# Adding the last pair's expert results with a gated selection matrix, and loading the gathered rows in two halves

## What is computed

```python
h = layer_norm(ALPHA * h + mix, ln_g[i, 0], ln_b[i, 0])        # layers 0 and 1
ffn = hier_moe(h, ...)      # gate_k * (silu(x @ w_gate[e_k]) * (x @ w_up[e_k])) @ w_down[e_k], k = 0, 1
h = layer_norm(ALPHA * h + ffn, ln_g[i, 1], ln_b[i, 1])
...
x = x + concat([att, lru_out]) @ w_out                         # layer 2
x = x + hierarchical_moe(rmsnorm(x, ffn_norm), ...)
return rmsnorm(x, final_norm)
```

## Time and profile before

| | us |
|---|---|
| median of 3 runs | 2155.4 (2151.24 to 2159.71) |
| profiled execution | 2147.33 |
| its span, first to last instruction | 2145.5 |
| PE busy in it | 1970.6 (92%) |
| DVE, ACT, POOL busy | 678.6, 404.3, 119.2 |
| mean granted clock of PE, 1 being 2.4 GHz | 0.968 |

### The profile page before, as it was taken

How to read it: one execution, slowest core, us unless ns; L and a number is a source line. 1 busy time by engine, 2 the same in 40 slices (tenths; PEclk the granted TensorE clock), 3 DMA queues, 4 the chain that set the end, 5 groups by cost and what they waited for, 6 DMA issues and landing times.

```text
span 2145.5 us, 25273 instructions
## 1 busy us (share of the span) xinstructions
PE 1970.6 (92%) x10013; PEld 1052.8 (49%) x10013; DVE 678.6 (32%) x1617; ACT 404.3 (19%) x873; POOL 119.2 (6%) x142
## 2 busy tenths in 40 slices
PE   8999989999999997799999999999499989999883
PEld 4444445555455453645545545544444445665442
DVE  0155547221111111535421111111637223532123
ACT  1033432111111111111111111111233222112112
POOL 0000001000000000000100000000010001111100
PEclk9999999999999999899999999999799999999997
DMA  9511103899999999722899999999821111699994
GB/s 318 152 57 40 40 20 114 356 419 420 420 421 421 420 419 372 273 83 79 313 419 420 421 420 421 421 419 404 287 84 40 39 40 41 217 366 418 419 419 200
DMA packets 122049, 593.93 MB, mean 277 GB/s; under 512 B 15915, under 2 KB 41403, under 8 KB 58991
## 3 DMA queue, kind: packets, MB, share of 16 engines
q1 hardware_dynamic: 108495, 565.96, 66.4%
q0 software_dynamic: 13472, 26.84, 3.8%
HBM read 573.48 MB, written 35.44 MB: 284 GB/s over the span
## 4 chain that ended last, share of the span: by engine, by line
PE 78%; DMA 14%; DVE 4%; ACT 2%; issue 1%; SPq 0%; DVEq 0%; POOLq 0%; ACTq 0%
PE bank L946 21%; PE bank L627 10%; PE bank L986 10%; PE bank L869 9%; DMA ring<-in_w_up_dram 6%; DMA ring<-in_moe_w_up_dram 6%; PE bank L769 4%; PE bank L639 4%; PE bank L613 3%; PE bank L1112 1%; PE bank L723 1%; PE bank L696 1%; PE bank L1073 1%; PE bank L860 1%; PE bank L683 1%
## 5 line engine op out<-in xcount | busy, mean ns | idle before, releaser
L946 PE MATMUL bank<-ring,work 128*64 128x512 f32 (+1 forms) x3008 | 562.5, 526 | 29.0 <-DMA ring<-in_w_up_dram 25.5
L946 PEld LDWEIGHTS bank<-ring,work 128*64 128x64 f32 x3008 | 224.8, 138 | 362.8 <-issue 335.3
L986 PE MATMUL bank<-ring,work 128*64 128x512 f32 x1280 | 295.9, 600 | 5.3 <-DVE work L1748 5.3
L1748 DVE COPY work<-bank 128x256 f32<-128x256 f32 (+1 forms) x96 | 36.5, 380 | 703.7 <-PE bank L861 703.7
L869 PE MATMUL bank<-work 128*128 128x128 f32 x2048 | 245.7, 278 | 0.0
L627 PE MATMUL bank<-hT,ring 128*128 128x512 f32 x512 | 236.9, 605 | 0.7 <-ACT work L1175 0.7
L869 PEld LDWEIGHTS bank<-work 128*128 128x128 f32 x2048 | 233.5, 192 | 6.1 <-issue 2.0
L1264 ACT ACTIVATE work<-bank 64x512 f32<-64x512 f32 x96 | 56.6, 589 | 540.8 <-PE bank L986 540.8
L986 PEld LDWEIGHTS bank<-ring,work 128*64 128x64 f32 x1280 | 84.3, 136 | 145.3 <-issue 129.1
L627 PEld LDWEIGHTS bank<-hT,ring 128*128 128x128 f32 x512 | 94.0, 193 | 109.1 <-issue 107.3
L1254 ACT ACTIVATE work<-bank 64x512 f32<-64x512 f32 (+1 forms) x96 | 49.7, 517 | 477.2 <-PE bank L946 477.2
(11 more groups left out here) (291 smaller groups left out, 1632.2 us busy)
## 6 DMA issues: line engine op xcount, KB each, us to landing
ring<-in_moe_w_down_dram SPq DMA_DIRECT2D x128, 1024.0 KB, 16.5
ring<-in_moe_w_gate_dram SPq DMA_DIRECT2D x126, 1024.0 KB, 15.4
ring<-in_moe_w_up_dram SPq DMA_DIRECT2D x126, 1024.0 KB, 17.2
ring<-in_w_down_dram SPq DMA_DIRECT2D x32, 1024.0 KB, 26.1
ring<-in_w_gate_dram SPq DMA_DIRECT2D x31, 1024.0 KB, 23.0
ring<-in_w_up_dram SPq DMA_DIRECT2D x31, 1024.0 KB, 24.9
ring<-in_attn_w_qkv_dram SPq DMA_DIRECT2D x12, 1024.0 KB, 13.7
work<-y_rows SPq DMA_DIRECT2D x12, 1024.0 KB, 8.0
```

Of the source, the lines that this page charges most:

```text
L946: mm = pe.matmul(GU2[s % 2][BLK * a:BLK * a + BLK, 0:F], xgT[pair % 2][:, per * kk + k, BLK * of_pair:BLK * of_pair + BLK], v[a][:, k, :], ...
L986: mm = pe.matmul(DN[BLK * n:BLK * n + BLK, :], hT_[:, 2 * kk + k, :], v[:, k, 512 * n:512 * n + 512], start=(kk + k == 0), stop=(2 * kk + ...
```

## The change

The results of the last two experts (30 and 31) are no longer stored to `y_rows`.

- ACT writes them to `last_y`, 128 rows by 1024. DVE builds a selection matrix for this pair, `last_sel`, whose entries are the gates (`select_last`, in slot 27); PE turns it (`turn_last_selection`, slot 29, four transposes); DVE copies it to `last_sum`. After the last expert PE computes for each tile two matmuls of 128 by 512 columns (`sum_last_pair`), and DVE adds them to `h` from the banks (`add_last`). The gates of choices that went to this pair are set to zero in `wts`; `y_rows` is filled with zeros once at the start, 4 MB.
- SP loads tiles 0 and 1 of the rows when the first 15 pairs' stores have landed, then issues the next projection's four units, then loads tiles 2 and 3. In layer 2 all four tiles are loaded in one go at that point.
- `project_turned` issues the sums of tiles 0 and 1 ahead of its loop, those of tiles 2 and 3 after the projection of tiles 0 and 1. ACT's order is not touched.
- DVE combines tiles 0 and 1 first, then adds the last pair tile by tile.
- In layer 2 the last pair's rows are gathered by matmuls like those of the first pairs, since the gated selection needs the selection matrix; `over_slots` has one turn ahead of its loop and two behind it in all layers.
- Two parameter semaphores are joined into one.

```diff
@@ load_tiles, after_gather (SP)
+            sp.dma_start(y_rows.rearrange("(p n) (q c) -> p (n q) c", p=P, c=256),
+                         zeros[:, :].unsqueeze(1).to_broadcast([P, 2 * S // P * 4, 256])).then_inc(rows_zeroed, 16)
...
-            def load_tiles(l):
+            def load_tiles(l, tiles):
                 sp.wait_ge(over_moved, l + 1)
-                for y_stored in steps.y_stored:
-                    sp.wait_ge(y_stored, 16 * (E // 4) * (l + 1))
-                for tt in range(T):
+                for y_stored, n in zip(steps.y_stored, STORES):
+                    sp.wait_ge(y_stored, 16 * n * (l + 1))
+                for tt in tiles:
...
-            def after_gather(l, u0, u1):
-                load_tiles(l)
+            def after_mixture(l, u0, u1, u2):
+                load_tiles(l, range(2))
+                for u in range(u0, u1):
+                    load(u)
+                load_tiles(l, range(2, T))
                 for tt in range(T):
                     sp.wait_ge(routing.gathered[tt], 16 * (l + 1))
-                for u in range(u0, u1):
+                for u in range(u1, u2):
                     load(u)
...
-            for u in range(first["pin"], first["pgrp"]):
-                load(u)
-            after_gather(0, first["pgrp"], first["moe1"])
+            after_mixture(0, first["pin"], first["pgrp"], first["moe1"])
@@ PE
+            def sum_last_pair(l, tt):
+                for n in range(2):
+                    mm = pe.matmul(last_bank(l, tt, n)[:, :], last_sum[:, P * tt:P * tt + P],
+                                   last_y[:, 512 * n:512 * n + 512], start=True, stop=True)
+                mm.then_inc(last_added, 1)
...
+            def project_turned(l, name, src, u0):
                 s = turns[name]
+                sum_last_pair(l, 0)
+                sum_last_pair(l, 1)
                 for tt in range(T):
                     turn(name, src, K, range(tt, tt + 1))
...
+                    if tt + 2 < T:
+                        sum_last_pair(l, tt + 2)
...
+                pe.wait_ge(main.xT, main.x0 + E + 1)
+                pe.wait_ge(main.ysb, main.n0 + E)
+                if l == 2:
+                    for tt in range(T):
+                        sum_last_pair(l, tt)
@@ ACT
+                    y = last_y if in_last else ysb[s // 2]
@@ DVE
+            def add_last(l, tt):
+                dve.wait_ge(last_added, T * l + tt + 1)
+                for n in range(2):
+                    hs = h[:, tt, 512 * n:512 * n + 512]
+                    ins = dve.tensor_tensor(hs, hs, last_bank(l, tt, n)[:, :], ALU.add)
...
+                    if type(i) is int and j == E - 5:
+                        select_last()
+                    if type(i) is int and j == E - 3:
+                        dve.wait_ge(main.xt, main.x0 + E + 1)
+                        dve.tensor_copy(last_sum, XT[0][:, :]).then_inc(main.xT, 1)
...
-            combine_tile(0, 0, 0)
-            combine_tile(0, 0, 1)
+            for tt in range(2):
+                combine_tile(0, tt, 0)
+                combine_tile(0, tt, 1)
+            add_last(0, 0)
             tile_variance(0)
             for tt in range(T):
                 if 1 <= tt < T - 1:
                     combine_tile(0, tt + 1, 0)
                 tile_normal(tt, 1, tiles_written, turns["ffn0"].src0)
                 if tt + 1 < T:
-                    if tt == 0:
-                        combine_tile(0, 1, 0)
-                    combine_tile(0, tt + 1, 1)
+                    if tt:
+                        combine_tile(0, tt + 1, 1)
+                    add_last(0, tt + 1)
                     tile_variance(tt + 1)
@@ POOL
-                for q in range(E // 2):
+                for q in range(E // 2 - 1):
```

More of the change, by code:

```diff
@@ L304, in turn_bank, with over_slots @@
             return bank[(2 * tt + kk) % 8]
-        def over_slots(eng, l, slot):
-            front, back = (2, 1) if l == 2 else (1, 2)
-            for s in range(front * TURN):
-                slot(s // TURN, s % TURN)
-            with eng.Fori(front, E // TURN - back) as i:
+        def over_slots(eng, slot):
+            for s in range(TURN):
+                slot(0, s)
+            with eng.Fori(1, E // TURN - 2) as i:
                 for s in range(TURN):
                     slot(i, s)
-            for s in range(back * TURN):
-                slot(E // TURN - back + s // TURN, s % TURN)
+            for s in range(2 * TURN):
+                slot(E // TURN - 2 + s // TURN, s % TURN)
         def last_slot(i, s):
@@ L1001, in mixture @@
                         turn_rows(m.ov, 0, 1, BLK)
-                        expert(m.ov, j, xgT[0][:, :, 0:BLK], 2 * j + 2, lambda q: ring[(m.base + q) % UNITS][:, :],
+                        expert(m.ov, j, xgT[1][:, :, 0:BLK], 2 * j + 2, lambda q: ring[(m.base + q) % UNITS][:, :],
                                lambda q: pe.wait_ge(m.ov_units, 16 * m.upb * j + 16 * m.upb))
+                    pe.wait_ge(m.ov.ysb, count)
+                pe.wait_ge(main.xT, main.x0 + E + 1)
+                pe.wait_ge(main.ysb, main.n0 + E)
+                if l == 2:
+                    for tt in range(T):
+                        sum_last_pair(l, tt)
             mixture(0, lambda k, tt: hT[:, k - 4, P * tt:P * tt + P])
-            project_turned("ffn0", h, first["pin"])
+            project_turned(0, "ffn0", h, first["pin"])
             u = first["pgrp"]
@@ L1755, in slot @@
                         product(i, s + 1)
[L1756 removed]
+                    if s % 2 == 0 and (0 < j < E - 5 and (l < 2 or j == E - 6) if type(i) is int else l < 2):
                         select(s // 2, j + 4)
@@ L1812, in _ @@
             mixture(1)
-            combine_tile(1, 0, 0)
-            combine_tile(1, 0, 1)
+            for tt in range(2):
+                combine_tile(1, tt, 0)
+                combine_tile(1, tt, 1)
+            add_last(1, 0)
             tile_variance(0)
```

117 lines of the change are left out of this document (78 added, 39 removed).

## The result

The changed kernel takes **2164.4 us** (median; the kernel before 2155.0 beside it), ratio 1.004, 95% interval 1.0025 to 1.0055: some 9 us slower, where the prediction said 1 us faster with nothing measurable as the likeliest. The profiled execution took 2158.9 us with a span of 2157.1, against 2147.3 and 2145.5 before.

What follows compares the result with a forecast made beforehand. PE was taken as the bound, idle at the mixtures' ends, with DVE the path in layer 2's; -2.0 (layer 0), +0.7 (layer 1), +1.5 (clock), -1.1 (layer 2), called -1, from 2155.4 gave 2154.4 us, range 2140 to 2166.

Steps and rivals of the forecast that it cites:

- The start of the projection: Ends of layers 0 and 1: early tile loads start PE's first projection 11.7 us earlier in layer 0, 11.8 in layer 1.
- The units: Ends of layers 0 and 1: the projection's four weight loads, now behind two tile loads, arrive in time; no cost.
- The rings: Layers 0 and 1's ends: two projections each wait through DVE and ACT for the next tile's sum, 6.1 and 7.6 us.
- The clock: Ends of layers 0 and 1: PE drops to 1.2 GHz in the new gaps; one of four rings charged, 1.5 us.
- the second rival: Ends of layers 0 and 1: the rings form and PE falls to 1.2 GHz in each; 2164 us, chance 0.14.
- layer 2's lag: Layer 2's last slots: gathering the last pair by matmuls delays PE, taken as 2.7 us between 0.8 and 6.6.
- Layer 2: Layer 2's end: DVE bounds the path from store to last step, which starts 1.1 us earlier despite the lag.
- The first, no rings: Ends of layers 0 and 1: a tile pays only PE's 1.7 us for its sum; 2137.6 us, chance 0.18.
- The third, early loads that don't come early: Layer ends: SP's first two tile loads are held until the last expert is done; 2175 us, chance 0.06.
- Small parts: Zero fill, selection work on DVE, four transposes in slot 29 and the stores left out: all at 0.

Runs made afterwards that it cites:

- all gaps filled: The changed kernel with matmuls of constants in all of PE's gaps at the ends of layers 0 and 1; ratio 0.9992 to the kernel before.
- the second execution: The changed kernel run and profiled once more, unaltered; ratio 1.0054 to the kernel before, span 2167.4 us.
- the zero fill alone: The kernel before plus only the change's 4 MB zero fill at the start; ratio 0.9981 to the kernel before.
- the kernel without rings: The changed kernel with ACT's copies ahead of the next root and, in layer 1, DVE's RMS step ahead of the next tile's work; 2136.1 us, ratio 0.9914.
- units first: The kernel without rings, with all four tile loads put behind the projection's four units; ratio 0.9994 to the kernel before.
- layer 2 as before: The changed kernel with layer 2's last pair gathered, stored and loaded as in the kernel before; ratio 1.0045 to the kernel before.
- ScalarE's order alone: The changed kernel with only ACT's copies put ahead of its roots, DVE's order kept; ratio 0.9972 to the kernel before.

## Why the prediction was wrong, step by step

**The start of the projection: right, 0.9 us too early.** The first turn stood at 9.8 us behind the last down product and came at 10.6, the first projection at 14.6 and came at 15.5 (866.19 - 850.71). The loads' issue, 6.1 us ahead of that product's end, was exact. What was short is tile 1's landing: it came 3.4 us behind tile 0 (4.8 and 7.8 us after issues 0.4 us apart), not 2.5, with the units right behind the two tiles, and DVE does all four sums ahead of the first add. (The prediction reads the 6.1 us between the shortest and the longest of the earlier trace rows as the distance of the landings; the issues are 1.3 us apart besides, so it is 7.4 us, and the 2.5 us a tile taken from it is right.) In layer 1 the first turn came 14.2 us behind the last down product, where 14.8 had been forecast. The units cost nothing, as forecast: the first two landed at 858.8 and 859.3, ahead of the projection at 866.19.

**The rings: right.** 6.1 us were forecast in layer 0, and 6.07 and 6.06 seen, by the very links that the prediction named; in layer 1 7.6 against 7.54 with PE warm.

**The clock: the step that failed.** "I put one of the four rings at that price, 1.5 us." The kernel with all gaps filled puts the whole price of the clock at 3.9 us in layer 0 and 6.4 in layer 1. Part of it the sum had already, since the first projection of each layer starts cold in the kernel before too. Behind the rings' waits the rows have: in layer 0 8.78 us for 7.41 in one ring of two, 1.4 us; in layer 1 9.10 and 9.16 for 7.41, and 8.0 for 7.54 in each ring by its cold turn, 4.4 us. That is **5.7 us where 1.5 stood**, and 9.1 us in the second execution, in which all four rings paid; by this term alone the forecast gain of 1 us turns into a loss. Besides, the first projections took 9.73 us for the 8.7 that the prediction took in layer 0 and 8.98 for 8.13 in layer 1, 1.9 us more. These vary without any ring too (9.12 and 9.39 us with the zero fill alone), so that they come from the change is not shown. With both the sums close: 60.5 - 2.0 + 0.9 (the start) + 1.4 + 1.0 = 61.8, seen 61.6; 62.0 + 0.7 - 0.6 (the start) + 4.4 + 0.8 = 67.3, seen 67.3. It is the term, and not the mechanism, that was mis-sized. By it the second rival came true; that it also hit the time (2164 forecast, 2164.4 measured) is partly chance, for it charged all four rings and 0.9 us a turn, where three of four paid in this profile and a cold turn lengthened the path by 0.5, and it took 5 us for layer 2's lag, which was 3.9. The reason given for the low price was that the rows showed a fall after such a gap once and a hold once. That was a tie, and a tie charged over four rings is two of them at least, not one; nor were layer 1's cold turns in the price, 0.5 us each: 1.5 us was the low end and no middle. The Trainium skill's rule ("TensorE: Matmul & The Clock Gate", HAM oscillation), that bursts with such waits between them each start at the lower clock, is borne out for five of the six in the changed kernel's first profile; the sixth, layer 0's second ring, held at 1.00 behind the same 3.31 us. In the second execution all six bear it out.

**Layer 2: right within 1 us.** The lag came out at 3.9 us (pair 14's store 247.1 us after the layer's first gate_up, 243.2 before), where 2.7 was taken between 0.8 and 6.6. From the last store to DVE's first sum it is 8.1 us (8.2 forecast), and from there to the last step 20.7 (21.0). POOL's and DVE's timelines, beside the earlier trace rows:

```profile
2124.32 0.97 POOL L2090 DMA_INDIRECT y_rows<-work,y_row  x1 [14.89 <-ACT work L1304]
...
2132.44 5.25 DVE L1428 SCALAR_TENSOR_TENSOR h<-work,h 128x1024 f32<-128x1024 f32 x4 [3.18 <-DMA work<-y_rows]
...
2153.16 1.41 DVE L1474 SCALAR_TENSOR_TENSOR work<-h,small,work 128x512 f32<-128x512 f32 x2
```

**The rivals.** The first, no rings, gave 2137.6 us; the kernel whose engines' order was mended measures 2136.1. Its price for a kernel without rings was right, its claim that the change as written has none was not. The third, early loads that don't come early, didn't occur; put into the kernel without rings by hand (units first) such a delay costs 10.4 and 12.0 us at the two ends, for the 8.0 that the prediction priced, since the tiles then also queue behind the units.

**Small parts: right.** The zero fill costs nothing that can be measured (0.9981, 0.9950 to 1.0013), and the loops over experts are within 1 us of before (470.1 and 470.8, for 469.3 and 470.8).

**Not settled.** The two ends lengthen the two profiled executions by 6.4 and 10.1 us, and the medians differ by 9.4. So no loss outside the ends is needed. But that the untouched stages were 0.7 and 3.0 us longer in one profile of the changed kernel and 3.7 and 7.5 in the other, and 0.7 and 8.3 longer with the zero fill alone, is explained only in part: in 100 us of "to g2" the granted clock was 0.85 with the zero fill alone (from 1656) and 0.90 in the profile of before (from 1650), with PE busy for 92.4 us in both. What decides in which execution the clock falls, and whether 2147.3 for the profile of before, 8 us under its median, was such a case of luck, these runs do not tell.

## What to carry to other kernels

When a piece of work is split so that a later engine's step waits for an earlier engine's *next* step, write down the order on each in-order engine and look for a ring: here the order of a few steps on ACT and DVE made 9 us of loss into 19 us of gain. Put the step that frees the bottleneck engine (the copy, the scaling of this tile) ahead of the step that waits for it (the root, the add for the next tile). And price each new wait of TensorE of the length seen here, 3.3 us or more between matmuls, with the slower start behind it: 1.4 to 2.9 us for a projection of 7.4 and 0.5 for a cold turn ahead of it, together more than the change won.

## What the runs showed of the hardware

- Of six waits of 3.31 us ahead of a projection (layer 0's rings in the changed kernel's two executions and with layer 2 as before) four were followed by a long one (8.78 to 10.35 us) and two by one of 7.41. Which of the two rings of an execution was hit changed: the first, both, the second. All eight waits of 4.32 us ahead of a turn (layer 1's rings, in these and with ScalarE's order alone) were followed by a turn of 1.97 and a projection of 8.9 to 9.3 us.
- Waits of TensorE broken up by matmuls on constants, so that none was longer than 1.4 us, kept the granted clock at 1.00 through both ends; the matmuls cost nothing there, as the rings' lengths (6.06 and 7.54 us) show.
- In code that no edit touched, one execution lost some 6.5 us from 358 to 375, where its granted clock was 0.50 in 360 to 370; the kernel without rings and the changed kernel had 0.83 there, the kernel with all gaps filled 0.66.
- Two tile loads of 1 MB issued 0.4 us apart, with 4 MB right behind them, landed 3.4 us apart in layer 0 and 2.7 in layer 1, and 4.1 in layer 1 of another execution; four with nothing behind them in the queue landed 2.5 us one after the other (4.8, 6.9, 8.9 and 10.9 us after issues 0.4 to 0.5 apart). That the 4 MB are the cause is not shown.
